# Forgetting attention: where the next unit's scores stand among the five key blocks of a head's shortest unit

## What is computed

```python
cum = jnp.swapaxes(jnp.cumsum(log_f, axis=1), 1, 2)
for i in range(lp // Q_BLOCK):
    lo, hi = i * Q_BLOCK, (i + 1) * Q_BLOCK
    s = einsum('bqhd,bkhd->bhqk', q[:, lo:hi], k[:, :hi]) * (HEAD_DIM ** -0.5)
    s = s + cum[:, :, lo:hi, None] - cum[:, :, None, :hi]
    mask = (idx[None, :hi] <= idx[lo:hi, None]) & key_valid[None, :hi]
    p = jax.nn.softmax(jnp.where(mask, s, -jnp.inf), axis=-1)
    outs.append(einsum('bhqk,bkhd->bqhd', p, v[:, :hi]))
```

## Time and profile before

| | |
|---|---|
| median of 3 runs | 2441.41 us (2439.84 to 2442.6) |
| profiled execution | 2440.79 us, span 2439.1 us |
| mean granted TensorE clock | 0.95 |
| TensorE matmuls busy | 2194.7 us, 90% |
| VectorE busy | 1712.5 us, 70% |
| ScalarE busy | 1489.1 us, 61% |
| GpSimd busy | 328.3 us, 13% |

### The profile page before, as it was taken

The page is one execution under the profiler, slowest core; times in us unless marked ns, Lnnn a source line. Parts: engine busy times, 40 slices in busy tenths (PEclk is TensorE's granted clock), DMA queues, the critical chain, the costliest instruction groups (busy, mean ns, idle before and its releaser), DMA issues. The chain is left out here.

```text
span 2439.1 us, 35900 instructions
## 1 busy us (share of the span) xinstructions
PE 2194.7 (90%) x11296; PEld 1787.6 (73%) x11296; DVE 1712.5 (70%) x3164; ACT 1489.1 (61%) x2262; POOL 328.3 (13%) x433
## 2 busy tenths in 40 slices
PE   7999999878789999999989995799999999999980
PEld 6788888655467777777768884688888888788860
DVE  5323231278588888888733346899999999999976
ACT  4323241276577777677633331778888788788867
POOL 0112111100000000000000000222222222222211
PEclk9999999979999999999989996899999999999995
DMA  6536352633341222222033424897887969998838
GB/s 199 179 108 188 111 186 78 172 68 95 104 107 38 68 70 59 70 68 78 18 109 142 150 113 155 293 377 258 272 290 212 300 209 354 325 306 301 271 99 297
DMA packets 220554, 420.62 MB, mean 172 GB/s; under 512 B 47912, under 2 KB 97144, under 8 KB 219288
## 3 DMA queue, kind: packets, MB, share of 16 engines
q1 hardware_dynamic: 187760, 316.08, 38.5%
q0 software_dynamic: 31648, 101.89, 14.5%
q10 hardware_dynamic: 1040, 1.31, 0.2%
HBM read 437.68 MB, written 86.39 MB: 215 GB/s over the span
## 5 line engine op out<-in xcount | busy, mean ns | idle before, releaser
L2476 DVE TENSOR_TENSOR moe_w_lo<-fetch_w_raw,moe_w_hi 128x1024 fp32r<-128x1024 f32 x376 | 435.3, 1218 | 9.7 <-ACT moe_w_hi L2405 9.6
L2405 ACT ACTIVATE moe_w_hi<-fetch_w_raw 128x1024 fp32r<-128x1024 f32 x376 | 368.3, 1052 | 61.2 <-DMA fetch_w_raw<-in_w_e_up_dram 28.6
L2530 PE MATMUL moe_ps_gu<-moe_w_hi,moe_xT_hi 128*128 128x512 f32 x736 | 293.4, 399 | 4.1 <-DVE moe_xT_lo L2487 4.1
L2532 PE MATMUL moe_ps_gu<-moe_w_hi,moe_xT_lo 128*128 128x512 f32 x736 | 289.2, 393 | 0.0
L2531 PE MATMUL moe_ps_gu<-moe_w_lo,moe_xT_hi 128*128 128x512 f32 x736 | 288.6, 392 | 0.0
L1438 ACT ACTIVATE fox_p_hi<-fox_ps_t 128x512 fp32r<-128x512 f32 (+4 forms) x352 | 181.0, 530 | 108.0 <-PE fox_ps_t L1578 107.2
L1505 DVE TENSOR_TENSOR fox_p_lo<-fox_ps_t,fox_p_hi 128x512 fp32r<-128x512 f32 (+4 forms) x352 | 211.0, 611 | 28.8 <-ACT fox_p_hi L1438 27.6
L1578 PE MATMUL fox_ps_t<-ident,fox_s 128*128 128x128 f32 (+1 forms) x1216 | 199.7, 279 | 30.4 <-ACT fox_s L1431 19.5
L2482 DVE TENSOR_TENSOR moe_d_lo<-fetch_d_raw,moe_d_hi 128x1024 fp32r<-128x1024 f32 x184 | 213.0, 1220 | 10.7 <-ACT moe_d_hi L2413 10.7
L1492 DVE CUSTOM_DVE_ANT_0 fox_s<-fox_ps_r,fox_ncum 128x512 f32<-128x512 f32 (+4 forms) x352 | 193.6, 569 | 20.0 <-PE fox_ps_r L1563 12.9
L1431 ACT ACTIVATE fox_s<-fox_s,fox_ntop 128x144 f32<-128x144 f32 (+5 forms) x192 | 173.4, 904 | 47.8 <-DVE fox_ntop L1500 47.2
(11 more groups left out here) (342 smaller groups left out, 4994.2 us busy)
## 6 DMA issues: line engine op xcount, KB each, us to landing
fetch_w_raw<-in_w_e_gate_dram SPq DMA_DIRECT2D x192, 512.0 KB
fetch_w_raw<-in_w_e_up_dram SPq DMA_DIRECT2D x192, 512.0 KB
fetch_d_raw<-in_w_e_down_dram SPq DMA_DIRECT2D x92, 1024.0 KB
ahead_raw<-in_w_in_dram SPq DMA_DIRECT2D x24, 1024.0 KB, 5.3
gates_wide<-in_x_dram SPq DMA_DIRECT2D x16, 512.0 KB
h<-gates_wide POOLq DMA_DIRECT2D x16, 512.0 KB, 3.3
gates_wide<-qT SPq DMA_DIRECT2D x32, 256.0 KB, 4.4
mix_h<-h SPq DMA_DIRECT2D x16, 512.0 KB, 3.6
```

Of the source, the lines that this page charges most:

```text
L2405: nc.scalar.activation(w_hi[:, k], w_raw[:, k].rearrange("p j n -> p (j n)"), ACT.Copy).then_inc(gu_high, 1)
L2476: nc.vector.tensor_tensor(w_lo[:, k], w_raw[:, k].rearrange("p j n -> p (j n)"), w_hi[:, k].bitcast(F32), ALU.subtract).then_inc(gu_split, 1)
L2530: nc.tensor.matmul(out, xT_hi[:, slot, k], w_hi[:, k, cols], start=k == 0, stop=False)
L2532: done = nc.tensor.matmul(out, xT_lo[:, slot, k], w_hi[:, k, cols], start=False, stop=k == KT - 1)
```

## The change

For a unit n with g = 0, the score half of unit n+1 is spread over 0 to 0.45 instead of 0 to 0.7. In the other units, and ahead of the first, nothing changes. No function, tile or instruction is added or removed.

```diff
-            SPREAD = 0.7
             for n in range(-1, UNITS):
                 events = []
+                spread = 0.45 if n >= 0 and units[n][1] == 0 else 0.7
                 if n + 1 < UNITS:
                     g = units[n + 1][1]
                     ahead = range(rows_before[n + 1], rows_before[n + 2])
-                    rate = SPREAD / len(ahead)
+                    rate = spread / len(ahead)
                     events += [(rate * (i + 0.5), "scores", r) for i, r in enumerate(ahead)]
                     for j in range(4):
                         done = sum(len(row_chunks(4 * g + i)) for i in range(j + 1))
                         events.append((rate * (done + 0.4), "tops", 4 * (n + 1) + j))
                         mine = [r for r in range(pieces_before[n + 1], pieces_before[n + 2]) if pieces[r][1] == j]
-                        events += [(rate * (done + 0.8) + 0.14 * SPREAD * (i + 0.5) / len(mine), "exp", r)
+                        events += [(rate * (done + 0.8) + 0.14 * spread * (i + 0.5) / len(mine), "exp", r)
                                    for i, r in enumerate(mine)]
```

## The result

The changed kernel takes 2427.61 us (median of 4 runs, 2425.75 to 2431.13) where the kernel before, run beside it, takes 2440.62 (4 runs): ratio 0.9949, 95% interval 0.9936 to 0.9962, 13.0 us less. Two later comparisons of the same pair, each with more runs, gave 0.9965 (0.9953 to 0.9976; 2432.45 against 2439.33) and 0.9951 (0.9935 to 0.9968; 2426.04 against 2439.3): 6.9 us between the medians in the one (8.5 by its ratio), 13.3 in the other (12.0 by its ratio). The first comparison is 12.4 by its ratio, so by the ratios the change is worth some 8 to 12 us. It was forecast as 2436.2, 5.2 us less, with a range that ended at 2430.5.

The account below looks back on a forecast made before the run. Bound in the g = 0 units: the chain VectorE (fourth maximum), ScalarE (exponential, copy), TensorE (products, turn_back). 2440.79 - 4.15 (moved work) - 1.0 (clock) = 2435.6, plus 0.6 for the median: 2436.2 us, range 2430.5 to 2441.

Parts of the forecast that it names:

- the moved work: Forgetting attention, g = 0 units: reordering gives 0.45 us a head in seven heads, 1.0 in head 0, 4.15 us in all.
- the clock: TensorE's granted clock falling to 1.2 GHz in the heads: a tenth of the 11.9 us lost is saved, 1.0 us.
- VectorE's step: p_lo of blocks 0 and 1 go behind the fourth maximum, which comes 0.79 us earlier in each g = 0 unit.
- ScalarE's step: Exponential 4 follows its maximum almost at once, p_hi of block 2 costs 0.28 us, the copy of oT comes 0.51 earlier.
- the bill: Time the kernel before loses to the granted clock's falls to 1.2 GHz in the heads: 11.9 us.
- The stretch of little work: TensorE turning 16-wide tiles, standing and multiplying with 16 rows before a clock fall: 3.0 us, to become some 2.7.
- Rival 2: The clock stays up in most heads: 2431.3 us with half the loss saved, 2425.4 with all; chance 0.20.
- Rival 1: The reordering gives its 4 us, the clock nothing or a cost up to 3: 2437.3 to 2440 us; chance 0.22.
- Rivals 3 and 4: 3: reorder moves nothing, 2440.5 to 2442 us, 0.12; 4: late p_lo of block 0 holds next meta block, 2447, 0.06.
- rival 4: Late p_lo of block 0 holds the next meta block and TensorE's in-order queue: slower, 2447 us; chance 0.06.
- the hole split in three: TensorE's 1.41 us wait becomes about 0.6 and 0.3; the wait before the 16-row product grows from 0.25 to 0.5.
- the late p_lo of block 2: VectorE's idle time appears before p_lo of block 2 and goes before p_lo of block 3, where 1.03 us of idle was.

Follow-up runs that it names:

- the kernel before with filled holes: Kernel before plus six TensorE products that nothing reads, five ahead of the meta tiles' turning and one ahead of the 16-row product: 2431.12 us against 2440.01.
- ScalarE alone: Kernel before with only ScalarE in the new order, VectorE and TensorE in the old: 2448.38 us against 2439.33.
- 0.55: Changed kernel with spread 0.55 in place of 0.45: 2437.19 us, kernel before 2439.05.
- TensorE alone: Kernel before with only TensorE in the new order, VectorE and ScalarE in the old: 2436.59 us against 2439.33.
- VectorE and TensorE: Kernel before with these two engines in the new order, ScalarE in the old: 2436.98 us against 2439.05.
- VectorE alone: Kernel before with only VectorE in the new order, ScalarE and TensorE in the old: 2429.54 us against 2439.33.
- 0.35: Changed kernel with spread 0.35 in place of 0.45: 2433.17 us, kernel before 2439.05.
- copy earlier: Changed kernel with the copy of oT ahead of p_hi of block 2 in the g = 0 units: 2419.98 us, kernel before 2440.01.
- filled: TensorE products that nothing reads added where it stands: kernel before 2431.12 us, changed kernel 2421.55, changed kernel with the copy of oT moved ahead 2421.62.

## Why the prediction was wrong

The steps of the moved work and their signs were right, and each is in the rows. Two terms of the sum were too small: the clock's, 1.0 us where 4.5 to 6.6 came, and the moved work's, 4.15 where some 6.3 came.

**VectorE's step.** Forecast: fourth maximum 0.79 us earlier, from 0.60 + 0.47 less 2 x 0.14. Measured 5.30 - 4.36 = 0.94. The subtraction of two p_lo was right; the gap behind a chunk costs about 0.1 us net, because maximum 3 wins back what one of the others loses, which I had seen and counted for nothing.

**ScalarE's step.** Forecast: exponential 4 starts almost without waiting, p_hi of block 2 costs 0.28, copy 0.51 earlier. Measured: no wait, 0.26, copy 0.67 earlier.

**The term of the moved work.** I then wrote 0.45 for a head, "since one more small wait is likelier than none". None reached the interval. The interval without a fall shows 67.85 - 67.1 = 0.75 us; the last 0.08 beside the 0.67 is time that I didn't follow up. Seven heads give 5.25 us where I had 3.15. Head 0: the part of the stage up to head 1's copy is 1.6 to 2.2 us shorter in the three profiles (83.68 us before; 81.65, 81.51 and 82.06), of which 0.75 belongs to head 1: 0.9 to 1.4, forecast 1.0. This part has falls of its own, with 17.1 us at 1.2 GHz before and 20.5, 17.1 and 20.5 after; where they are equal the difference is 1.4. The moved work is worth some 6.3 us, not 4.15.

**The term that failed most: the clock.** Forecast 1.0 us: a tenth of the bill, because the hole was to be a tenth shorter. The bill itself was right: the kernel before with filled holes is 8.9 us faster, and some of its falls had only gone elsewhere. Wrong was the size of the hole after the change, and perhaps its measure. The stretch of little work was to shrink from 3.0 us to 2.7 and shrank to 2.4 (from 1083.72, where the first wait begins, to the next full-width product at 1086.08). TensorE's idle time inside it went from 1.41 + 0.25 = 1.66 us to 0.24 + 0.19 + 0.53 = 0.96, 42% less; the prediction's own signs (0.6, 0.3 and 0.5) add up to 1.4, so it had the waits before the thin tiles too long, above all the first, 0.6 for 0.24. The falls did not become a tenth rarer; in the three profiles none of 6.8 us (2.4 to 2.5 us of time each) is left behind a short unit, only falls of 3.4 us (1.05 each) or none. In the first profile the bill went from 11.9 to 5 x 1.05 = 5.25, in the second to 7 x 1.05 = 7.35. Moved work 6.3 plus clock 4.5 to 6.6 gives 10.8 to 12.9. The stage says the same in each profile: 12.9 worked out and 13.1 measured in the first, 10.8 and 11.1 in the second, 12.9 and 12.6 in the third. The three comparisons say 12.4, 8.5 and 12.0. The 8.5 lies below: executions of the kernel before differ by up to 10 us (2435.26 to 2445.2), a spread that the rest of the program alone can make (1877.0 to 1890.2 us), and my one profile of it need not have the mean bill. How the bill is spread over executions was not measured.

Why a shorter hole gives shorter falls stays open. Over all profiles the time at 1.2 GHz behind the short units of heads 1 to 7 goes roughly with TensorE's idle time around the thin work: 44 us at 1.92 us of idle time (ScalarE alone), 31 to 34 at 1.3 to 1.7 (the kernel before, 0.55, TensorE alone, VectorE and TensorE), 20 and 27 at 1.15 and 1.10 (VectorE alone, 0.35), 17, 24 and 17 at 0.95 (the changed kernel), 7 at 0.68 (copy earlier), none at 0.26 or less (filled). It is one profile each but for the changed kernel, and not a proportion: falls of 6.8 us are there at 1.10 us.

**The rivals.** Rival 2 had 0.20. Its price came nearest, half of the bill saved and 2431.3 us, but not its condition: the clock does not stay up in most heads, it falls in five, seven and five of seven, for half as long. Rival 1, nothing from the clock and 2437.3 to 2440, is out: all three medians lie below it. Rivals 3 and 4 are out: p_lo of block 0 does hold the first meta tiles, by 0.24 us, and the exponential still comes 0.19 us later than they are done. Something like rival 4, another engine's queue held up, showed itself where one engine has the new order and another the old: of the 0.7 us a head that ScalarE alone loses, 0.4 is the later fourth maximum, with VectorE's wait of 0.30 us in it.

**The page's rule.** The Trainium skill, page "TensorE: Matmul & The Clock Gate", section "A second HAM failure mode: psum-queue depth-cycling", says that short idle times between groups of matmuls are enough to make the clock swing. The traces agree: with three holes of at most 0.53 us it still falls in 17 of 21 short units. What the prediction drew from it, that cutting the hole up gives nothing back, did not come, since the falls were shorter; but the hole was not only cut up, its idle time went down as well.

**What would show it.** The wait of exponential 4 gone, the hole split in three, the late p_lo of block 2: all there, though the first two parts of the hole are shorter than listed. The interval was to be 67.4 and is 67.1, and the prediction had named that as a sign of being wrong. The count of heads at 1.2 GHz changed little (from six to five, seven and five), as I had asked for: I had watched the number of falls, not their length.

## What to carry to other kernels

Where a loop has the same short hole on TensorE in each round, write down the intervals of the rounds and the granted clock behind each hole: here equal work took 67.85, 68.85 and 70.35 us, and the clock's part was larger than the hole. Count how long each fall lasts, not only how many there are, look at the idle time in the hole and not at the length of the stretch alone, and test it at once by filling the hole with products that nobody reads. Compare the stage as well as the total: the untouched rest of this kernel varied by 13 us. And when the order of a shared list is changed, look for what now stands in each queue ahead of the one instruction that the others wait for: one p_hi ahead of the copy was worth 0.26 us a head, and taking it out of the way brought the lowest median of this study, together with fewer falls (two in its profile).

## What the runs showed of the hardware that was not expected

With a hole of 1.66 us in all and the same instructions in each head, the time at 1.2 GHz behind it was 6.8, 3.4 or 0 us and no value between; with 0.96 us it was 3.4 or 0 in all of 21 cases. Filling the hole removed the fall at the hole, but in two kernels the clock then fell 12 us later, in two heads and in six, behind a stand of 1.01 us. The same stand had no fall behind it in the kernel before (one head) and in the changed kernel with its holes filled (six heads). In the changed kernel seven heads in a row had the same fall, at intervals of 68.12 to 68.20 us, and in another execution two of seven had none. What decides whether a given hole brings a fall was not found.
